# Gated recurrences: when the value and gate products of a pair of heads run, beside its own scores

## The reference

```
def _hgrn2_mixer(h, w_in, g_norm, w_out, lb):
    q, zf, zb, i, g = jnp.split(h @ w_in, 5, axis=-1)
    ...
    def forget(z):
        logf = jnp.logaddexp(log_lb, log_1m_lb + jax.nn.log_sigmoid(to_heads(z, HG_DK)))
        return 1.0 - jnp.exp(logf), logf
    k_f, logf_f = forget(zf)
    k_b, logf_b = forget(zb)
    qh = to_heads(q, HG_DK) * (HG_DK ** -0.5)
    vh = to_heads(i, HG_DV)
    ...        # fwd + bwd: sum over s of (q_t . decay(t, s) . k_s) v_s, in both directions
    gh = g.reshape(B, T, HG_HEADS, HG_DV).astype(jnp.float32)
    o = _rms_norm(o, g_norm) * jax.nn.silu(gh)
    return o.reshape(B, T, D_MODEL).astype(h.dtype) @ w_out
```

## Time and profile before

| | |
|---|---|
| median of three runs | 2884.41 us |
| profiled execution, its own time | 2884.56 us |
| its span, first to last instruction | 2882.7 us |
| mean granted TensorE clock | 0.992 |
| TensorE busy (matmul) | 2800.3 us, 97% |
| VectorE busy | 1951.7 us, 68% |
| ScalarE busy | 1439.9 us, 50% |
| chain that ended last | TensorE 88%, VectorE 6%, ScalarE 3%, issue 2% |
| DMA | mean 166 GB/s |
| PSUM scores of layer 0, first to last | 232.3 to 386.0 us |
| the same of layer 3 | 1883.1 to 2037.9 us |

### The profile page before, as it was taken

One profiled execution on the slowest core, in us unless ns is written; L12 is line 12 of the kernel. 1 busy time (PEld: TensorE's weight loads), 2 busy tenths in 40 slices (PEclk: granted clock), 3 DMA queues, 4 the chain that ended last, 5 costly groups with the idle time before them and its releaser, 6 DMA issues.

```text
span 2882.7 us, 48145 instructions
## 1 busy us (share of the span) xinstructions
PE 2800.3 (97%) x20356; PEld 2594.5 (90%) x20356; DVE 1951.7 (68%) x2547; ACT 1439.9 (50%) x1970; POOL 94.5 (3%) x147
## 2 busy tenths in 40 slices
PE   9999989999998999999999999999899999999998
PEld 8999879999996999998889999998799989988997
DVE  5757876565665656556665565588755788767877
ACT  5445554444456444445644444456444644455543
POOL 0000000000012000001100000000000100000000
PEclk9999999999999999999999999999999999999999
DMA  7654436676552665663346556443465456554563
GB/s 245 205 162 147 124 120 195 190 211 184 160 171 64 202 183 175 195 187 95 108 139 185 175 191 188 154 147 111 139 194 187 151 180 207 179 161 139 175 214 102
DMA packets 406282, 478.46 MB, mean 166 GB/s; under 512 B 16634, under 2 KB 332820, under 8 KB 406068
## 3 DMA queue, kind: packets, MB, share of 16 engines
q1 hardware_dynamic: 404244, 469.07, 51.7%
q0 software_dynamic: 1632, 6.25, 0.8%
q10 hardware_dynamic: 192, 0.08, 0.0%
HBM read 474.29 MB, written 1.05 MB: 165 GB/s over the span
## 4 chain that ended last, share of the span: by engine, by line
PE 88%; DVE 6%; ACT 3%; issue 2%; POOL 0%; DMA 0%; ACTq 0%; POOLq 0%; DVEq 0%
PE Wk L710 18%; PE Wk L712 18%; PE Wk L711 18%; PE Y L710 10%; PE Y L711 10%; PE Y L712 9%; DVE w_lo L2000 2%; DVE work L2300 1%; PE Y L819 1%; PE Wk L1090 1%; ACT w_hi L1425 1%; PE Y L1000 1%; PE Y L1074 0%; PE Wk L1074 0%; PE Y L1103 0%
## 5 line engine op out<-in xcount | busy, mean ns | idle before, releaser
L2000 DVE TENSOR_TENSOR w_lo<-ring,w_hi 128x1024 fp32r<-128x1024 f32 (+2 forms) x910 | 1068.1, 1199 | 560.9 <-ACT w_hi L1425 516.9
L710 PE MATMUL Wk<-xT_hi,w_hi 128*128 128x256 f32 x4320 | 1230.0, 285 | 6.9 <-DVE w_lo L2000 3.5
L712 PE MATMUL Wk<-xT_hi,w_lo 128*128 128x256 f32 x4320 | 1222.3, 283 | 0.0
L711 PE MATMUL Wk<-xT_lo,w_hi 128*128 128x256 f32 x4320 | 1222.2, 283 | 0.0
L1425 ACT ACTIVATE w_hi<-ring 128x1024 fp32r<-128x1024 f32 (+1 forms) x894 | 906.9, 1039 | 596.9 <-PE Wk L712 420.0
L710 PEld LDWEIGHTS Wk<-xT_hi,w_hi 128*128 128x128 f32 x4320 | 828.3, 192 | 18.1 <-issue 7.0
L711 PEld LDWEIGHTS Wk<-xT_lo,w_hi 128*128 128x128 f32 x4320 | 828.5, 192 | 4.7 <-issue 1.0
L712 PEld LDWEIGHTS Wk<-xT_hi,w_lo 128*128 128x128 f32 x4320 | 828.4, 192 | 0.0
L710 PE MATMUL Y<-w_hi,hid_hi 128*128 128x512 f32 x936 | 369.1, 394 | 5.0 <-issue 3.0
L711 PE MATMUL Y<-w_lo,hid_hi 128*128 128x512 f32 x936 | 366.5, 392 | 0.0
L712 PE MATMUL Y<-w_hi,hid_lo 128*128 128x512 f32 x936 | 365.4, 390 | 0.0
(11 more groups left out here) (308 smaller groups left out, 2658.3 us busy)
## 6 DMA issues: line engine op xcount, KB each, us to landing
ring<-in_ffn_w_gu SPq DMA_DIRECT2D x352, 512.0 KB, 4.5
ring<-in_ffn_w_down SPq DMA_DIRECT2D x224, 512.0 KB, 4.2
ring<-in_ffn_w_up SPq DMA_DIRECT2D x96, 512.0 KB, 6.0
ring<-in_hg_w_in SPq DMA_DIRECT2D x80, 512.0 KB, 3.7
ring<-in_na_w_in SPq DMA_DIRECT2D x24, 512.0 KB, 4.5
ring<-in_hg_w_out SPq DMA_DIRECT2D x16, 512.0 KB, 3.3
ring<-in_lru_w_in SPq DMA_DIRECT2D x16, 512.0 KB, 4.1
ring<-in_kv_w SPq DMA_DIRECT2D x16, 512.0 KB, 5.1
```

What stands on the lines that cost most here:

```text
L710: pe.matmul(o, l_hi, r_hi, start=first, stop=False)
L711: pe.matmul(o, l_hi, r_lo, start=False, stop=False)
L712: return pe.matmul(o, l_lo, r_hi, start=False, stop=last)
L2000: ins = dve.tensor_tensor(l, r, h.bitcast(F32), ALU.subtract)
```

## The change

The stream of halves is shifted by four (HG_LEAD = 6): only z and q of a pair are made before its first score. Halves 6 to 9 of a pair (values, gate) run behind scores 0 to 3 of **the same** pair, halves 0 to 4 of the next pair behind scores 4 to 8, and half 5 after the last. In the last pair halves 6 to 9 run behind scores 0 to 3, and the four output halves behind scores 4 to 7.

Everything that hangs on the halves moves with them. VectorE: `save_g` and its clamp (now a function of its own, `clamp_g`) from i = 0 to i = 4, `gate_of` from i = 2 to i = 6, `save_z` of the next pair from i = 4 to i = 8, and `bounded`, `save_q` (now behind `bounded`), `start_queries`, `both_ways` all to i = 8. In the last pair `save_g` stands first in step 4. ScalarE: `save_values` to i = 2 of the pair itself, `g_sigmoid` from i = 1 to i = 5, `z_sigmoid` and `one_minus` of the next pair all to i = 8. `squares_summed` goes from i = 4 to i = 5, `roots` from 5 to 6, `normed` from 6 to 7 (in the last pair these stay). The splits keep their distance of four units ahead of TensorE.

```diff
-HALVES_LAST = (0, 0, 1, 1, 2, 2, 3, 4, 5)
+HALVES_LAST = (-2, -1, 0, 1, 1, 2, 3, 4, 5)
+HG_LEAD = 6
...
@@ TensorE
-                for i in range(4, 10):
+                for i in range(4, HG_LEAD):
                     half_product(0, i)
                 for p_ in range(HG_PAIRS):
                     last = p_ == HG_PAIRS - 1
                     for i in range(SCORES):
                         score(p_, i)
+                        if last and i == 0:
+                            output(p_ - 1)
+                        if last and i == 1:
+                            squares_summed(p_ - 1)
                         if not last:
-                            half_product(p_ + 1, i)
-                        if p_ and i == 2 - 2 * last:
+                            half_product(*divmod(10 * p_ + HG_LEAD + i, 10))
+                        elif i < 4:
+                            half_product(p_, HG_LEAD + i)
+                        if p_ and not last and i == 2:
                             output(p_ - 1)
-                        if p_ and i == 4 - 3 * last:
+                        if p_ and not last and i == 5:
                             squares_summed(p_ - 1)
-                        if last and i in (0, 2, 4, 6):
-                            pair_out(i // 2 % 2, i // 4)
+                        if last and 4 <= i < 8:
+                            pair_out(i % 2, (i - 4) // 2)
                     if not last:
-                        half_product(p_ + 1, 9)
+                        half_product(p_ + 1, HG_LEAD - 1)
...
@@ ScalarE
+                one_minus(Q0)
                 splits(base[s] + 4)
-                one_minus(Q0)
-                splits(base[s] + 5)
-                save_values(0)
-                splits(base[s] + 6)
...
-                        if i == 1:
+                        if i == 2:
+                            save_values(p_)
+                        if i == 5:
                             g_sigmoid(Q)
                         if not last:
-                            ahead(HALVES_AHEAD + 10 * (p_ + 1) + i, s)
+                            ahead(HALVES_AHEAD + 10 * p_ + HG_LEAD + i, s)
...
-                        if p_ and i == 5 - 3 * last:
+                        if p_ and i == 6 - 4 * last:
                             roots(p_ - 1)
                         if not last:
-                            if 4 <= i < 7:
-                                z_sigmoid(Q + 1, i - 4)
-                            elif i == 7:
+                            if i == LEVELS:
+                                for part in range(3):
+                                    z_sigmoid(Q + 1, part)
                                 one_minus(Q + 1)
-                            elif i == LEVELS:
-                                save_values(p_ + 1)
...
@@ VectorE
                 save_z(0)
-                splits(base[s] + 4)
+                bounded(0)
                 save_q(0)
-                bounded(0)
-                splits(base[s] + 5)
                 start_queries(0)
                 both_ways(0)
                 multiply_blocks(Q0, LEVELS - 1)
-                splits(base[s] + 6)
+                splits(base[s] + 4)
                 for p_ in range(HG_PAIRS):
                     Q, last = Q0 + p_, p_ == HG_PAIRS - 1
                     for i in range(SCORES):
+                        if last and i == 4:
+                            save_g(p_)
...
-                        if i == 0:
+                        if i == 4 and not last:
                             save_g(p_)
-                        elif i == 2:
+                            clamp_g(p_)
+                        if i == 4 and last:
+                            clamp_g(p_)
+                        if i == 6 + 0 * last:
                             gate_of(p_)
...
-                        if p_ and i == 6 - 3 * last:
+                        if p_ and i == 7 - 4 * last:
                             normed(p_ - 1)
                         if not last:
-                            ahead(HALVES_AHEAD + 10 * (p_ + 1) + i, s)
-                            if i == 4:
+                            if i == LEVELS:
                                 save_z(p_ + 1)
-                            elif i == 6:
+                            ahead(HALVES_AHEAD + 10 * p_ + HG_LEAD + i, s)
+                            if i == LEVELS:
+                                bounded(p_ + 1)
                                 save_q(p_ + 1)
-                            elif i == 7:
-                                bounded(p_ + 1)
                                 start_queries(p_ + 1)
-                            elif i == LEVELS:
                                 both_ways(p_ + 1)
                                 multiply_blocks(Q + 1, LEVELS - 1)
```

More of the change, by code:

```diff
@@ L2246, in save_g, with clamp_g @@
                         .then_inc(g_saved, 1)
+                def clamp_g(p_):
+                    Q = Q0 + p_
                     dve.wait_ge(g_saved, Q + 1)
```

## The result

The changed kernel took 2906.82 us (median of three, 2906.43 to 2907.74) against 2884.41 us: 1.0076 times as long, 95% interval 1.0062 to 1.009. The profiled execution is the one of 2906.43 us; its span is 2904.6 us and its mean granted TensorE clock 0.988 against 0.992.

What follows compares the result with a forecast made beforehand. TensorE was taken to bound nearly everything. Per stage 4.3 + 10.5 - 7.7 = +7.1 us; in all 2884.6 + 2 x 7.1 - 1.5 + 10.5 = 2907.8, said as 2908, range 2890 to 2920.

Steps and rivals of the forecast that it cites:

- waits at the three ends: TensorE idle before score 0 of the next pair, waiting for the z and q chains: 3.3, 4.7 and 4.7 us.
- late scores, pairs 0 to 2: Scores before each pair's end held up by VectorE's queue: 2.3 us in pair 0, 0.5 and 0.5 after.
- late scores, last pair: In the last pair score 4 is 0.5 us late, scores 7 and 8 are 0.8 and 0.5 late.
- wait for the gate: Last pair: the output half behind score 4 waits for VectorE's `save_g`, 3.6 us idle.
- end of the last pair: Idle time that stays: 0.7 us before the last output and an estimated 1.6 before the last tile.
- half clock behind the five: Lower TensorE clock after each stage's five waits; seven of ten in both stages priced at 1.5 us, 10.5 in all.
- Part 1: Four weight halves move into the last pair: of 15.4 us lost there 7.7 remain, a gain of 7.7 per stage.
- Part 4: Clock falls behind the new waits cost 10.5 us, bounds 0 and 15; an old fall of 1.5 goes away.
- Part 2: Stage start: two halves instead of six cover the way from z to the first score, costing 4.3 us idle.
- Part 3: Each pair's end: z and q complete later, so TensorE waits and scores are late, +10.5 us per stage.
- Rival B: The waits come in the two recurrent stages but the clock holds: 2897 us, chance 0.19.
- Rival D: Gain and cost cancel, with shorter end waits, half the lateness and half the clock falls: 2887 us, chance 0.12.

Runs made afterwards that it cites:

- e2_gate: The changed kernel with VectorE saving the last pair's gate in step 3 behind the block product, not at the head of step 4: 2898.77 us.
- e4_last: The changed kernel with the last pair as before the change, its four value and gate halves ahead of its scores: 2907.81 us.
- e5_lead8: The changed kernel with the stream shifted by two halves, not four; values stand before the pair's first score, only the gate streams behind its scores: 2848.86 us.
- e1_clock: The changed kernel with idle products on TensorE in its five long waits of each stage: 2885.37 us.
- e3_normed: The changed kernel with the normalisation moved on VectorE from step 7 into step 8's wait for the sigmoid, in pairs 1 and 2: 2899.47 us.
- e7_before_clock: The kernel before the change with idle products in its last pair alone, behind scores 3, 5 and 7: 2873.96 us.
- e6_all: The changed kernel with the last pair's gate saved early, the normalisation in the sigmoid's gap, and idle products in the remaining four waits: 2878.46 us.

## Why the prediction was right

2907.8 was forecast and 2906.8 measured, but the closeness is partly luck: two terms were off, in opposite directions. The idle times were counted too long, by 5.4 and 5.1 us in the two stages, and the half clock too short, by 4.0 and 4.8.

| term, first stage | predicted, us | measured |
|---|---|---|
| wait at the start | 4.3 | 4.05 |
| waits at the three ends | 3.3, 4.7, 4.7 | 3.02, 4.34, 4.32 |
| late scores, pairs 0 to 2 | 2.3, 0.5, 0.5 | 1.2, 0, 0 |
| late scores, last pair | 0.5, 0.8, 0.5 | 0.15, 0.34, 0 |
| wait for the gate | 3.6 | 3.24 |
| end of the last pair | 0.7, 1.6 | 0.69, 1.38 |
| half clock behind the five | 5.25 | 9.2 |

- **Part 1, the last pair.** Mechanism and place right: e2_gate shows the gate's wait to be VectorE's queue and e4_last's trace shows the gain to be real. Idle time left is 5.8 us instead of 7.7. Without the clock, which Part 4 prices, the gain was 15.4 - 5.8 = 9.6 us instead of 7.7.
- **Part 2, the start.** Right to 0.25 us; the row names `both_ways` as releaser. Nothing undid this term alone; e5_lead8, which puts two halves back, has no wait there.
- **Part 3, the ends.** Right in order and nearly in size. VectorE reached z's save 2.2 us late in pair 1 (z complete at 301.99 by the ninth score's start, saved from 304.20) instead of 2.9, and 0.9 in pair 0 (257.32 to 258.26) instead of 1.4. What was off is the count of VectorE's queue. The four steps of pair 1 that were counted as 4.5, 5.5, 4.0 and 4.0 us took 4.2, 5.4, 3.65 and 3.7, 1.0 us less in all. The records of the instructions in them overlap by about 0.1 us each (257.13 + 1.23 = 258.36, and the next starts at 258.26), which was not taken off. Two sums are also 0.1 off (2.2 + 2.9 - 0.3 is 4.8, not 4.7; 2.8 + 2.2 + 1.4 + 1.2 + 0.7 is 8.3, not 8.4), which changes nothing.
- **Part 4, the clock.** The mechanism was right, the term mis-sized: seven falls of 1.5 us were priced, 10.5 us; ten came, of 1.4 to 2.7 us each, 19.2 us in all by the steps and 20.2 by e1_clock. The 1.5 came from a single fall of some 3 us. Five of the ten here went on for twice as long, from 266.2 to 273.1 us for one; these five began before TensorE had resumed. The earlier trace rows had such a dear fall already, 2.6 us on one output half. The Trainium skill ("TensorE: Matmul & The Clock Gate", "HAM oscillation — how this bites in real kernels") has the cost paid again at each burst behind a wait. The trace agrees: all ten waits paid. In e3_normed it does not: two of ten, of 3.44 and 3.42 us, paid nothing.
- The sum of 7.1 us per stage takes 4.4 us of old half clock off (2.6 and 1.8, in the 15.4), so it stands for 7.1 + 4.4 = 11.5 us of idle time; measured are 6.1 and 6.4. The clock was short by nearly as much, and the total came out right. Rival B (the clock holds), 2897, has the idle times too long as well: where the clock does hold, in e1_clock, the time is 2885.

Rival D had the terms cancel for this kernel, and they did not. What e5_lead8 shows is another thing: a shift of two instead of four keeps the gain and none of the cost.

## What to carry to other kernels

When filler work is moved from ahead of a chain to behind it, count what covers the chain's **last** producer: here q's products ended with nothing left to run, and 3.4 us of wait stayed when VectorE's order was mended (e3_normed). Try to move only as little as fills the empty place (two halves gave 1.3% where four cost 0.8%). Where TensorE must wait for some us, price the clock behind the wait as a term of its own, and try idle products there; they paid some 9 us even in the kernel before.

## What the runs showed of the hardware

- All ten waits of 3.0 to 4.3 us in the changed kernel were followed by a clock of 0.50. With waits of 3.4 us in e3_normed two such places kept 1.00, and the kernel before has one fall after 1.86 us, where e7_before_clock, unchanged in this place, has none after the same wait. So the length of a wait alone did not decide it in this range.
- Idle float32 products of 128 x 512 into a spare bank, ended 0.2 to 0.9 us before the wait did, kept the granted clock at 1.00 in all 24 places where they were put (ten in e1_clock, eight in e6_all, six in e7_before_clock).
- Consecutive VectorE instructions overlap in the records by about 0.1 us, which matters when a queue is summed.
